# A decoder-trunk step on one core: the MLP's channels in 16 chunks of 512 instead of 8 of 1024

## The reference

```python
hm = jnp.square(jax.nn.relu(rmsnorm(x, norm_mlp) @ w_up))   # w_up 2048 x 8192
x = x + hm @ w_down                                          # w_down 8192 x 2048
...
y = rmsnorm(x, norm_final)
```

## Time and profile before

| | |
|---|---|
| runs | 2255.88, 2256.86, 2258.83 us |
| span of the profiled execution | 2258.0 us |
| what lies around the span | under 1 us, since the longest run is 2258.83 us |
| TensorE matmul busy | 2176.6 us, 96% of the span |
| TensorE weight load busy | 2107.0 us, 93% (beside the matmuls) |
| VectorE busy | 1225.0 us, 54% |
| ScalarE busy | 780.7 us, 35% |
| GpSimd busy | 157.1 us, 7% |
| the 16 DMA engines | 137 GB/s on average |
| the MLP, by its first and last matmul | 1301.5 us to 2239 us from the span's start |

### The profile page before, as it was taken

One profiled execution on the slowest core, in us unless ns is written; L12 is line 12 of the kernel. 1 busy time (PEld: TensorE's weight loads), 2 busy tenths in 40 slices (PEclk: granted clock), 3 DMA queues, 4 the chain that ended last, 5 costly groups with the idle time before them and its releaser, 6 DMA issues.

```text
span 2258.0 us, 37515 instructions
## 1 busy us (share of the span) xinstructions
PE 2176.6 (96%) x14489; PEld 2107.0 (93%) x14489; DVE 1225.0 (54%) x1988; ACT 780.7 (35%) x938; POOL 157.1 (7%) x318
## 2 busy tenths in 40 slices
PE   6999998999999999999999999999999999999997
PEld 5999997899998899999999999999999999999996
DVE  5877677555566555555454454444434443444445
ACT  5334554222232222233334443333333232323342
POOL 3000001110022110010000100000000000000001
PEclk9999999999999999999999999999999999999998
DMA  5444344333353333336444444444444444444442
GB/s 163 140 149 149 117 139 131 106 113 102 121 160 122 113 117 112 100 122 205 149 149 150 148 143 156 145 155 132 149 132 149 131 150 133 151 133 152 148 145 93
DMA packets 294457, 309.04 MB, mean 137 GB/s; under 512 B 9584, under 2 KB 290288, under 8 KB 294080
## 3 DMA queue, kind: packets, MB, share of 16 engines
q1 hardware_dynamic: 290464, 291.54, 40.8%
q0 software_dynamic: 3584, 15.55, 2.3%
q10 hardware_dynamic: 288, 0.15, 0.0%
HBM read 298.83 MB, written 8.37 MB: 136 GB/s over the span
## 4 chain that ended last, share of the span: by engine, by line
PE 86%; DVE 6%; issue 3%; ACT 3%; DMA 0%; DVEq 0%; ACTq 0%; SPq 0%
PE main L1322 26%; PE main L1323 26%; PE main L1324 26%; PE aux L1418 6%; DVE scratch L804 2%; ACT hi L557 2%; DVE lo L804 1%; DVE scratch L811 1%; PE aux L1401 0%; PE aux L1391 0%; DVE scratch L808 0%; DVE scratch L807 0%; DVE merged L811 0%; DMA raw<-in_w_in 0%; PE aux L1360 0%
## 5 line engine op out<-in xcount | busy, mean ns | idle before, releaser
L804 DVE TENSOR_TENSOR lo<-raw,hi 128x1024 fp32r<-128x1024 f32 x546 | 668.9, 1233 | 601.1 <-ACT hi L557 595.0
L557 ACT ACTIVATE hi<-raw 128x1024 fp32r<-128x1024 f32 x546 | 573.1, 1056 | 964.1 <-PE main L1324 956.4
L1322 PE MATMUL main<-x_hi,hi 128*128 128x320 f32 x2688 | 848.3, 316 | 26.5 <-issue 12.6
L1323 PE MATMUL main<-x_lo,hi 128*128 128x320 f32 x2688 | 837.0, 311 | 0.0
L1324 PE MATMUL main<-x_hi,lo 128*128 128x320 f32 x2688 | 836.8, 311 | 0.0
L1322 PEld LDWEIGHTS main<-x_hi,hi 128*128 128x128 f32 x2688 | 510.4, 190 | 23.0 <-DVE qkv L804 9.7
L1323 PEld LDWEIGHTS main<-x_lo,hi 128*128 128x128 f32 x2688 | 510.7, 190 | 13.8 <-issue 13.2
L1324 PEld LDWEIGHTS main<-x_hi,lo 128*128 128x128 f32 x2688 | 510.2, 190 | 0.0
L1322 PE MATMUL main<-o_hi,hi 128*128 128x320 f32 x1408 | 442.1, 314 | 4.6 <-DVE o_lo L804 4.6
L1324 PE MATMUL main<-o_hi,lo 128*128 128x320 f32 x1408 | 435.6, 309 | 0.0
L1323 PE MATMUL main<-o_lo,hi 128*128 128x320 f32 x1408 | 435.5, 309 | 0.0
(11 more groups left out here) (225 smaller groups left out, 1173.9 us busy)
## 6 DMA issues: line engine op xcount, KB each, us to landing
raw<-in_w_in SPq DMA_DIRECT2D x210, 512.0 KB, 3.6
raw<-in_w_up SPq DMA_DIRECT2D x128, 512.0 KB, 3.6
raw<-in_w_down SPq DMA_DIRECT2D x128, 512.0 KB, 3.3
raw<-in_w_back SPq DMA_DIRECT2D x80, 512.0 KB, 3.3
scratch<-in_s_in POOLq DMA_DIRECT2D x8, 512.0 KB, 4.6
out_s_out<-scratch POOLq DMA_DIRECT2D x8, 512.0 KB, 4.6
merged<-in_x SPq DMA_DIRECT2D x4, 640.0 KB, 9.0
qkv<-in_x POOLq DMA_DIRECT2D x1, 2560.0 KB, 10.5
```

Source lines behind the costliest of these rows:

```text
L557: act.activation(HI[:, slot * TILE:(slot + 1) * TILE], RAW[:, slot * TILE:(slot + 1) * TILE], ACT.Copy).then_inc(hi_ready, 1)
L804: return dve.tensor_tensor(out, a, b, op)
L1322: pe.matmul(bank, hi, xh, start=first, stop=False)
L1323: pe.matmul(bank, hi, xl, start=False, stop=False)
```

## The change

A chunk is 512 channels: 8 up tiles (two strips) and 8 down tiles, each down tile alone accumulating its pair `d` over the chunk's 512 rows. There are 16 chunks; the first and the last are written out, the 14 between are a loop, which jumps back 13 times. `down_tile` goes away. Steps that fell on the same place in `walk` are joined: `relu2(1)` and `down(0)` both stand under 12. `down(5)`, `down(6)` and `down(7)` move into the next chunk. `OH` and `OL` are used in their first half alone.

```diff
-            with sp.Fori(0, 8) as it:
-                for j in range(16):
-                    load(MLP_N, 32, it, j, A["w_up"], j % 4 * 512, it * 1024 + j // 4 * 256)
-                for j in range(16):
-                    d = j // 4 * 2 + j % 2
-                    load(MLP_N, 32, it, 16 + j, A["w_down"], it * 1024 + j // 2 % 2 * 512, d * 256)
+            with sp.Fori(0, 16) as it:
+                for j in range(8):
+                    load(MLP_N, 16, it, j, A["w_up"], j % 4 * 512, it * 512 + j // 4 * 256)
+                for d in range(8):
+                    load(MLP_N, 16, it, 8 + d, A["w_down"], it * 512, d * 256)
...
             def relu2(it, s):
-                act.wait_ge(evacuated, it * 24 + (MLP_T + 2 * s + 2 + RING))
-                if not isinstance(it, int) or it * 4 + s:
-                    act.wait_ge(hm_ready, it * 4 + s)
+                act.wait_ge(evacuated, it * 20 + (MLP_T + 2 * s + 2 + RING))
+                if not isinstance(it, int) or it * 2 + s:
+                    act.wait_ge(hm_ready, it * 2 + s)
...
             def mlp(it, after):
-                ups_ = {8 + 4 * s: [lambda s=s: relu2(it, s)] for s in range(4)}
-                walk(split, MLP_N, 32, it, 32, {**ups_, **after})
+                ups_ = {8 + 4 * s: [lambda s=s: relu2(it, s)] for s in range(2)}
+                walk(split, MLP_N, 16, it, 16, joined(ups_, after))
...
             def relu2(it, s):
-                tile_done(MLP_N, 32, it, 4 * s + 3)
+                tile_done(MLP_N, 16, it, 4 * s + 3)
...
             def down(it, d):
-                tile_done(MLP_N, 32, it, down_tile(d))
+                tile_done(MLP_N, 16, it, 8 + d)
...
             def mlp(it, after):
-                own = {8 + 4 * s: [lambda s=s: relu2(it, s)] for s in range(4)}
-                own.update({down_tile(d) + 4: [lambda d=d: down(it, d)] for d in range(6)})
-                walk(split, MLP_N, 32, it, 32, {**own, **after})
+                own = {8 + 4 * s: [lambda s=s: relu2(it, s)] for s in range(2)}
+                own = joined(own, {12 + d: [lambda d=d: down(it, d)] for d in range(5)})
+                walk(split, MLP_N, 16, it, 16, joined(own, after))
...
             def mlp(it, between):
-                for s in range(4):
-                    strip(MLP_N, 32, MLP_T, 24, it, 4 * s, 2 * s, XH, XL, between=between,
+                for s in range(2):
+                    strip(MLP_N, 16, MLP_T, 20, it, 4 * s, 2 * s, XH, XL, between=between,
                           waits=(lambda i: (xg2_ready, 2 * (i + 1))) if isinstance(it, int) and it + s == 0 else None)
-                for j in range(16):
-                    d, half = j // 4 * 2 + j % 2, j // 2 % 2
-                    tile(MLP_N, 32, MLP_T, 24, it, 16 + j, 8 + 2 * d, 4 * half, 8, OH, OL,
-                         (hm_ready, it * 4 + 2 * (half + 1)) if j in (0, 2) else None)
+                for d in range(8):
+                    tile(MLP_N, 16, MLP_T, 20, it, 8 + d, 4 + 2 * d, 0, 4, OH, OL,
+                         (hm_ready, it * 2 + 2) if d == 0 else None)
...
-            with pe.Fori(1, 7) as it:
+            with pe.Fori(1, 15) as it:
                 mlp(it, {})
-            mlp(7, {})
+            mlp(15, {})
```

More of the change, by code:

```diff
@@ L520, in lru_steps @@
                     for pos, ks in ((3, (0,)), (4, (1,)), (5, (2, 3)), (6, (4,)), (7, (5,)))}
-        def down_tile(d):
-            return 16 + d // 2 * 4 + 2 + d % 2
         def dn_place(k, peeled):
@@ L776, in mlp @@
             def mlp(it, after):
-                ups_ = {8 + 4 * s: [lambda s=s: relu2(it, s)] for s in range(4)}
-                walk(split, MLP_N, 32, it, 32, {**ups_, **after})
+                ups_ = {8 + 4 * s: [lambda s=s: relu2(it, s)] for s in range(2)}
+                walk(split, MLP_N, 16, it, 16, joined(ups_, after))
             def last_squares(d):
-                act.wait_ge(evacuated, 7 * 24 + MLP_T + 8 + 2 * d + 2 + RING)
+                act.wait_ge(evacuated, 15 * 20 + MLP_T + 4 + 2 * d + 2 + RING)
                 act.wait_ge(sq2_used, 8 + d)
@@ L785, in _ @@
             mlp(0, {4: [lambda: residual(7)], 6: [lambda: root(4)]})
-            with act.Fori(1, 7) as it:
+            with act.Fori(1, 15) as it:
                 ch.enter(it, 1, LINKS["mlp"])
                 mlp(it, {})
[L789 to L792, removed]
+                ch.leave(14, "mlp")
+            mlp(15, {12 + d: [lambda d=d: last_squares(d)] for d in range(5)})
+            for d in range(5, 8):
+                last_squares(d)
             root(5)
@@ L1284, in relu2 @@
                         .then_inc(evacuated, 1)
-                dve.wait_ge(hf_ready, it * 4 + (s + 1))
+                dve.wait_ge(hf_ready, it * 2 + (s + 1))
                 c = slice(2 * s * N, 2 * (s + 1) * N)
@@ L1295, in mlp, with last_downs @@
             def mlp(it, after):
-                own = {8 + 4 * s: [lambda s=s: relu2(it, s)] for s in range(4)}
-                own.update({down_tile(d) + 4: [lambda d=d: down(it, d)] for d in range(6)})
-                walk(split, MLP_N, 32, it, 32, {**own, **after})
-            mlp(0, {4: [lambda: residual(3, 1)], 6: [rms_mlp]})
[L1301 to L1305, removed]
+                own = {8 + 4 * s: [lambda s=s: relu2(it, s)] for s in range(2)}
+                own = joined(own, {12 + d: [lambda d=d: down(it, d)] for d in range(5)})
+                walk(split, MLP_N, 16, it, 16, joined(own, after))
+            def last_downs(it):
+                return {d - 4: [lambda d=d: down(it, d)] for d in range(5, 8)}
+            mlp(0, {4: [lambda: residual(3, 1)], 6: [rms_mlp]})
+            with dve.Fori(1, 15) as it:
+                mlp(it, last_downs(it - 1))
+            mlp(15, last_downs(14))
+            for d in range(5, 8):
+                down(15, d)
             dve.wait_ge(sq2_used, 16)
@@ L1577, in mlp @@
             def mlp(it, between):
-                for s in range(4):
-                    strip(MLP_N, 32, MLP_T, 24, it, 4 * s, 2 * s, XH, XL, between=between,
+                for s in range(2):
+                    strip(MLP_N, 16, MLP_T, 20, it, 4 * s, 2 * s, XH, XL, between=between,
                           waits=(lambda i: (xg2_ready, 2 * (i + 1))) if isinstance(it, int) and it + s == 0 else None)
-                for j in range(16):
-                    d, half = j // 4 * 2 + j % 2, j // 2 % 2
-                    tile(MLP_N, 32, MLP_T, 24, it, 16 + j, 8 + 2 * d, 4 * half, 8, OH, OL,
-                         (hm_ready, it * 4 + 2 * (half + 1)) if j in (0, 2) else None)
+                for d in range(8):
+                    tile(MLP_N, 16, MLP_T, 20, it, 8 + d, 4 + 2 * d, 0, 4, OH, OL,
+                         (hm_ready, it * 2 + 2) if d == 0 else None)
             mlp(0, {3: [(7, lambda: sum_squares(8))]})
-            with pe.Fori(1, 7) as it:
+            with pe.Fori(1, 15) as it:
                 mlp(it, {})
-            mlp(7, {})
+            mlp(15, {})
             sum_squares(16)
-LINKS = {"qkv": 6, "lru": 8, "gpl": 4, "gpp": 6, "rglru": 1, "mlp": 4}
+LINKS = {"qkv": 6, "lru": 8, "gpl": 4, "gpp": 6, "rglru": 1, "mlp": 2}
 def kernel(x_prompt, x_sample, state_lru_h, state_lru_conv, state_dn_s, state_dn_conv, state_pool,
```

## The result

The changed kernel takes 2362.04 us, the median of four runs (2357.11 to 2362.56), against 2257.85 us for the kernel before in the same comparison. The ratio is 1.0451, with a 95% interval of 1.0436 to 1.0467. The change is slower by 104 us. The forecast was 2354 us, with a range of 2340 to 2376.

A forecast was written before the change was run, and what follows sets the result against it. The prediction took TensorE's matmuls, busy 96% of the span, as the bound. Wait 97.6 plus clock 33.6 minus removed jumps 34.35 gave +96.9 us on 2256.86, so 2354 us, range 2340 to 2376.

The forecast's parts named there:

- What bounds the kernel: TensorE's matmuls, busy 96% of the span; its ten MLP pauses lie at the loop's five jumps back.
- The jumps removed: Old TensorE MLP loop: five jumps back go away, 6.87 us each, saving 34.35 us.
- the second gap: TensorE's pause a few matmuls after the first jump's first gap, until 1533.85 us; also read as the branch.
- The jumps added: New TensorE MLP loop: 13 jumps of a half-as-long body, priced at 0; bounds 0 and 6.87 us each.
- The wait added: Tile 8 of each of 16 chunks waits for the squared strip 1: 6.1 us each, 97.6 us in all.
- The clock behind it: Slow matmuls at granted clock 0.50 after each of 16 pauses: 2.1 us each, 33.6 us in all.
- The sum: All terms together: 97.6 + 33.6 - 34.35 = +96.9 us, giving 2354 us, 4.3% slower.
- VectorE: 128 more residual adds, 62 us of VectorE time beside the down tiles, at cost 0.
- The covered chain: Rival: strip 1 is already squared when TensorE reaches tile 8, only jumps count; 2222 us, chance 0.02.
- The dear jumps of the new loop: Rival: the new loop's 13 jumps cost 6.87 us each, 89.3 us on top; 2443 us, chance 0.04.
- The rule of the Trainium skill: Only two 256-instruction blocks are held, so the new body of 768 would miss at each jump; set against the trace.
- The clock that doesn't fall: Rival: no slow matmuls behind the new pauses, +63.3 us; 2320 us, chance 0.04.

The follow-up runs named there:

- The steps up to 1468: Changed kernel with 120, 200, 300 or 350 unread matmuls between tiles 7 and 8 of each chunk: 2506.36, 2696.33, 2928.8 and 3049.07 us.
- the filled pause: Changed kernel with 36 unread matmuls put between tile 7 and tile 8 of each chunk: 2322.01 us, ratio 1.0282.
- The shortened chain: Changed kernel with relu2(1) ahead of the split of tile 11 on ScalarE and VectorE instead of behind it: 2309.74 us, ratio 1.0222.
- two chunks in a passage: Changed kernel with two chunks in each passage of TensorE's loop, 6 jumps and a body of 768 matmuls and 768 loads: 2395.02 us, ratio 1.0598.
- the moved strip: Changed kernel with the next chunk's first strip moved between this chunk's second strip and down product: 2234.89 us, ratio 0.9897.

## Why the prediction was right

*What bounds the kernel.* Right. The reading that all of TensorE's ten gaps in the MLP belong to the jumps was an assumption; writing the loop out confirmed it.

*The jumps removed*, 34.35 us. With the loop written out the MLP's stretch is 33.9 us shorter, so the term was right. By span it is 32.2 us, because the stretch from 360 to 400 us, where no jump is involved, was slower in that profile; by median it is 29.6 (2256.8 to 2227.16). That the branch's 4 us are the idle time was wrong for the second gap, as said above; the sum did not use it, since it took the whole price from the windows.

*The jumps added*, 0. Right: 208 ns in the median, and no change when the loop is written out. The argument was a comparison of body lengths with the loop at line 1531. The steps up to 1468 show that it held with much room.

*The wait added*, 6.1 us, bounds 5.97 and 6.4. Measured 5.91 in the loop, a little below the lower bound. The chain is the one read from the earlier trace rows, instruction for instruction; the register operation that I added for the loop costs next to nothing, since the waits are 91.9 us in all with it and 91.6 in the written-out form without it. The forecast said 90 to 96.

*The clock behind it*, 2.1 us. This is the term that was mis-sized: 2.5 us on average by the timeline and 2.4 by the filled pause, within its bounds of 1.6 and 3.1. I took the value of the jumps, where the idle time comes in two pieces and is 4 us in all. The shortened chain gives part of the reason: on average 1.55 us behind 3.7 us late, 2.5 behind 5.9. But the length of the pause doesn't fix the price. Behind equal pauses of 5.9 us it went from 1.5 to 2.6 us in the changed kernel, and from 1.4 to 2.8 with two chunks in a passage. What sets it within that range is open; the prediction's single value for all 16 pauses had no row behind it.

*The sum.* With the measured terms, 16 x (5.91 + 2.47) - 33.9 = 100.2 us, which is what the MLP's stretch grew by. The spans differ by 101.8 us, with the 1.6 us from ahead of the MLP, and the medians by 104.2 us; the interval of the ratio alone is plus or minus 3.5 us. The forecast of 96.9 had 6 us too little for the clock and 3 us too much for the wait. That the two misses partly cancel is luck.

*VectorE.* No cost, right: after the wait is covered the doubled adds hold nobody up. The 62 us of busy time that I forecast are 56.0, because the two adds of a pair overlap: a pair takes 0.88 to 0.9 us and not 0.97.

*The rivals.* The covered chain (2222 us) did not come by itself, but the moved strip makes it true on purpose, and the time is then 2234.89 us with one pause left. The dear jumps of the new loop (2443 us) did not come. The rule of the Trainium skill (Runtime: NRT & Kernel Launch, "Instruction fetch mechanics") that a jump beyond two blocks of 256 instructions has to fetch is not what these runs show on TensorE: 1507 instructions jump free. Its room for 2048 is not borne out as a limit for a loop body either, since the jump of 1575 is dear. The clock that doesn't fall (2320 us) is what the filled pause gives, 2322.01 us.

## What to carry to other kernels

Before a loop is cut into smaller pieces, look at which producer chain the old order had hidden, and read its length from the trace while it is still covered: the step from the last matmul to the last subtraction was there in full. Smaller pieces cost nothing here once one strip of other work lay between producer and consumer, and they gained what the shorter loop body saves. When TensorE is nearly always busy, price a pause as the idle time plus the slow matmuls behind it, here 5.9 + 2.5 us on average, and give the second part a range.

## What was not expected of the hardware

- The price of a jump is a step and not a slope: 208 ns up to 1468 matmuls and loads in the body, 4002 ns at 1536, and with the second gap behind the branch and the slow matmuls 6.6 us of time.
- The slow stretch behind a longer pause costs more on average (1.55 us behind a matmul that comes 3.7 us late, 2.5 us behind one that comes 5.9 us late, 0.1 us behind 0.65 us), but equal pauses of 5.9 us cost anything from 1.4 to 2.8 us.
- The same wait is called by its releaser (`DVE o_lo`) in a loop and "issue" in written-out code, and a gap made by a jump is put down to VectorE's adds. Only the first of these labels named the cause; the edit was what told.
